# State transfers issued by SyncE, and part of VectorE's work in the mLSTM state loop given to GpSimd

## The reference

```python
# per sample and head: state C is 512 x 512
C_new = decay * C + einsum('k,v->kv', wg * k, v)          # the samples' states, written out
h     = einsum('k,kv->v', q, C_new) / max(|den|, exp(-m))  # the samples' output
C_p   = einsum('sk,sv->kv', wg * k, v)                     # the prompt's state, written out
hc    = num / max(|den|, exp(-m))                          # the prompt's output, per head
mu, var = hc.mean(-1), mean((hc - mu)**2)
hn  = (hc - mu) * rsqrt(var + EPS) * ln_g
out = ((hn + skip * xc) * silu(z)) @ w_out
```

## Time and profile before

| | us |
|---|---|
| median of 3 runs | 2687.95 (2685.96 to 2688.54) |
| profiled execution | 2686.03 |
| its span, first to last instruction | 2683.9 |
| TensorE busy | 2429.1 |
| VectorE busy | 1805.6 |
| ScalarE busy | 1563.1 |
| GpSimd busy | 411.5 |

### The profile page before, as it was taken

One profiled execution on the slowest core, in us unless ns is written; L12 is line 12 of the kernel. 1 busy time (PEld: TensorE's weight loads), 2 busy tenths in 40 slices (PEclk: granted clock), 3 DMA queues, 4 the chain that ended last, 5 costly groups with the idle time before them and its releaser, 6 DMA issues. The chain is left out here.

```text
span 2683.9 us, 50227 instructions
## 1 busy us (share of the span) xinstructions
PE 2429.1 (91%) x17500; PEld 2195.1 (82%) x17500; DVE 1805.6 (67%) x3814; ACT 1563.1 (58%) x3012; POOL 411.5 (15%) x436
## 2 busy tenths in 40 slices
PE   6978999899977999998989978899999987999997
PEld 3658989888966999997766535898899976999997
DVE  6855698866698555557447784459885479655555
ACT  5644555577688555555526762355556569555554
POOL 0000344300043000000002331024440025000000
PEclk8989999999999999999998998999999999999999
DMA  6743444477601545453326995344444520445452
GB/s 231 259 134 141 157 157 157 173 258 259 234 16 33 187 174 185 178 182 133 98 80 265 417 324 185 129 156 157 157 170 172 186 80 0 151 178 184 176 186 96
DMA packets 74318, 455.79 MB, mean 170 GB/s; under 512 B 9680, under 2 KB 9888, under 8 KB 27632
## 3 DMA queue, kind: packets, MB, share of 16 engines
q1 hardware_dynamic: 52128, 379.61, 39.3%
q0 software_dynamic: 20336, 73.30, 7.3%
q10 hardware_dynamic: 1760, 1.68, 0.2%
HBM read 415.28 MB, written 39.27 MB: 169 GB/s over the span
## 5 line engine op out<-in xcount | busy, mean ns | idle before, releaser
L861 ACT ACTIVATE w_parts<-ring 128x512 fp32r<-128x512 f32 x1376 | 853.1, 632 | 804.2 <-PE ps L446 769.9
L1294 DVE TENSOR_TENSOR w_parts<-ring,w_parts 128x512 fp32r<-128x512 f32 x1232 | 853.9, 704 | 613.0 <-ACT w_parts L861 603.7
L446 PE MATMUL ps<-h_hi,w_parts 128*128 128x264 f32 x5376 | 1024.9, 289 | 84.9 <-DVE w_parts L1294 59.4
L446 PEld LDWEIGHTS ps<-h_hi,w_parts 128*128 128x128 f32 x5376 | 857.5, 192 | 114.7 <-issue 60.7
L446 PE MATMUL ps<-h_lo,w_parts 128*128 128x264 f32 x2688 | 771.9, 287 | 0.0
L446 PE MATMUL ps<-g_parts,w_parts 128*128 128x264 f32 x6144 | 748.5, 284 | 6.7 <-DVE g_parts L1594 6.7
L446 PEld LDWEIGHTS ps<-g_parts,w_parts 128*128 128x128 f32 x6144 | 748.2, 189 | 7.1 <-issue 7.1
L446 PEld LDWEIGHTS ps<-h_lo,w_parts 128*128 128x128 f32 x2688 | 516.6, 192 | 2.0
L1197 POOL TENSOR_TENSOR w_parts<-ring,w_parts 128x512 fp32r<-128x512 f32 x144 | 211.7, 1471 | 479.0 <-ACT w_parts L861 478.7
L861 ACT ACTIVATE SCR<-SCR 128x128 f32<-128x128 f32 (+3 forms) x540 | 212.5, 484 | 13.2 <-POOL SCR L1212 8.9
L446 PE MATMUL ps<-SCR 128*128 128x128 f32 x1056 | 155.8, 293 | 63.0 <-DVE SCR L1565 44.8
(11 more groups left out here) (188 smaller groups left out, 1569.4 us busy)
## 6 DMA issues: line engine op xcount, KB each, us to landing
ring<-in_stream SPq DMA_DIRECT2D x362, 1024.0 KB, 4.8
BIG<-in_C POOLq DMA_DIRECT2D x64, 512.0 KB, 8.6
out_C_s<-BIG POOLq DMA_DIRECT2D x64, 512.0 KB, 8.1
out_C_p<-SCR POOLq DMA_DIRECT2D x16, 256.0 KB, 7.5
x<-in_x ACTq DMA_DIRECT2D x1, 1056.0 KB, 15.3
out_y<-BIG POOLq DMA_DIRECT2D x1, 1056.0 KB, 4.2
consts<-in_consts ACTq DMA_DIRECT2D x1, 256.0 KB, 10.8
BIG<-in_gates POOLq DMA_DIRECT2D x1, 192.0 KB, 2.6
```

The lines of the kernel that those rows point to most:

```text
L446: return nc.tensor.matmul(out, lhsT, rhs, start=start, stop=stop, skip_group_check=shared)
L861: return nc.scalar.activation(to, of, f, **kw_)
L1294: tt(w_lo[:, j % HALVES, :], half_of(n, half), w_hi[:, j % HALVES, :].bitcast(F32), ALU.subtract).then_inc(lo_ready[half], 1)
```

## The change

The reciprocal of the denominators is taken head by head, each before its head's product. In the state loop:

- Loads and stores of the states and the store of `Cst` are issued by SyncE, in the same order with the same waits; the weight stream's SyncE program is cut up so that eight of its pairs are issued inside that sequence, one behind each store of `Cst`. `Cst` has one buffer instead of two.
- VectorE still adds the second terms of q C, into three buffers (`rd` with two, `rd_more`); GpSimd adds the two units' sums, and TensorE multiplies once for each iteration.
- The second half of each gate tile's low part is subtracted by GpSimd (`low_z`).
- VectorE joins the gain with the scaling at m = 24 and 25 (one instruction for each chunk); adding the skip part and multiplying with the gate is done by GpSimd, two chunks at a time (`finish_h`), from m = 25 on. ScalarE scales xc by `skip` at m = 16 to 23, two chunks at a time.

```diff
@@ sync @@
+            def rounds_of_pairs(first, end):
+                with sp.Fori(first, end) as r:
+                    for s in range(PAIRS):
+                        sp.wait_ge(pairs_used, r * PAIRS + (s - PAIRS + 1))
+                        pair(r * PAIRS + s, s)
+            def pairs(first, end):
+                for n in range(first, end):
+                    sp.wait_ge(pairs_used, n - PAIRS + 1)
+                    pair(n, n % PAIRS)
+            def load_C(u):
+                sp.dma_start(flat(Cbuf[u % CBUFS]), half_C(C_d, u)).then_inc(C_in[u % CBUFS], 16)
+            z0 = FIRST["ml_z"] // 2
+            ahead = z0 + PAIRS - 1
+            rounds_of_pairs(1, ahead // PAIRS)
+            pairs(ahead // PAIRS * PAIRS, ahead)
+            sp.wait_ge(qs_ready, 2)
+            sp.wait_ge(st_done, 1)
+            for u in range(CBUFS):
+                load_C(u)
+            LAG = 3
+            for u in range(UNITS):
+                sp.wait_ge(C_new, u + 1)
+                sp.dma_start(half_C(C_s_o, u), flat(Cbuf[u % CBUFS])).then_inc(C_out[u % CBUFS], 16)
+                if u % 4 == 3:
+                    n = u // 4
+                    sp.wait_ge(cp_copied, n + 1)
+                    sp.dma_start(C_p_o[n], Cst).then_inc(cp_stored, 16)
+                    if n < KM // 2:
+                        pairs(ahead + n, ahead + n + 1)
+                old = u - LAG
+                if old >= 0 and old + CBUFS < UNITS:
+                    sp.wait_ge(rd_ready, old + 1)
+                    sp.wait_ge(C_out[old % CBUFS], 16 * (old // CBUFS + 1))
+                    load_C(old + CBUFS)
+            ahead += KM // 2
+            again = -(-ahead // PAIRS)
+            pairs(ahead, again * PAIRS)
+            rounds_of_pairs(again, rounds)
+            pairs(rounds * PAIRS, NTILES // 2)
...
@@ tensor, read_C @@
-                for q in range(2):
-                    pe.wait_ge(rd_ready, 2 * m + q + 1)
-                    last = mm(ps[0:HEADS * NSMP, 4, :], one_col[:, at:at + HEADS * NSMP], rd[:, q, :],
-                              m == 0 and q == 0, m == NSMP * HEADS - 1 and q == 1)
-                    last.then_inc(C_read, 1)
+                pe.wait_ge(rd_summed, m + 1)
+                mm(ps[0:HEADS * NSMP, 4, :], one_col[:, at:at + HEADS * NSMP], rd[m % 2],
+                   m == 0, m == NSMP * HEADS - 1).then_inc(C_read, 1)
...
             pe.wait_ge(mly_ready, 1)
+            pe.wait_ge(hn_gated, KM // 2)
             residual_out("ml_out", hT, KM)
...
@@ scalar, scale_rd and the loop @@
+                act.wait_ge(C_new, 2 * m + 1)
+                if m >= 2:
+                    act.wait_ge(C_read, m - 1)
+                func(rd[m % 2], Cbuf[2 * m % CBUFS][:, 0, :], ACT.Copy, scale=qs[:, hd * HC, b:b + 1])\
+                    .then_inc(rd_scaled, 1)
+                act.wait_ge(C_new, 2 * m + 2)
+                if m >= 1:
+                    act.wait_ge(rd_summed, m)
+                func(rd_more, Cbuf[(2 * m + 1) % CBUFS][:, 0, :], ACT.Copy, scale=qs[:, hd * HC + 2, b:b + 1])\
+                    .then_inc(rd_scaled, 1)
...
-                    if n >= 2:
-                        act.wait_ge(cp_stored[n % 2], 16 * (n // 2))
-                    func(Cst[:, n % 2, :], ps[:, 5 + n % 2, :], ACT.Copy).then_inc(cp_copied, 1)
-                if m < KM:
-                    func(xc[:, m, :], xc[:, m, :], ACT.Copy, scale=col("ml_skip", m)).then_inc(skip_ready, 1)
+                    if n >= 1:
+                        act.wait_ge(cp_stored, 16 * n)
+                    func(Cst, ps[:, 5 + n % 2, :], ACT.Copy).then_inc(cp_copied, 1)
+                if KM <= m < KM + KM // 2:
+                    for c in (2 * (m - KM), 2 * (m - KM) + 1):
+                        func(xc[:, c, :], xc[:, c, :], ACT.Copy, scale=col("ml_skip", c)).then_inc(skip_ready, 1)
...
@@ gpsimd @@
+            def low_z(k):
+                j = HALF["ml_z"] + 2 * k + 1
+                pool.wait_ge(hi_ready, j + 1)
+                nc.gpsimd.tensor_tensor(w_lo[:, j % HALVES, :], half_of(FIRST["ml_z"] + k, 1),
+                                        w_hi[:, j % HALVES, :].bitcast(F32), ALU.subtract).then_inc(lo_ready[1], 1)
+            def sum_rd(m):
+                pool.wait_ge(rd_ready, 2 * m + 2)
+                nc.gpsimd.tensor_tensor(rd[m % 2], rd[m % 2], rd_more, ALU.add).then_inc(rd_summed, 1)
+            def finish_h(k):
+                pool.wait_ge(hn_ready, 2 * k + 2)
+                pool.wait_ge(skip_ready, KM)
+                of = (slice(None), slice(2 * k, 2 * k + 2), slice(0, NPR))
+                nc.gpsimd.tensor_tensor(hT[of], hT[of], xc[of], ALU.add).then_inc(hn_skipped, 1)
+                pool.wait_ge(hn_skipped, k + 1)
+                nc.gpsimd.tensor_tensor(hT[of], hT[of], z[of], ALU.mult).then_inc(hn_gated, 1)
+            pool.wait_ge(lo_ready[1], HALF["ml_z"] // 2)
+            for k in range(2):
+                low_z(k)
+            for m in range(NSMP * HEADS):
+                if m >= 1:
+                    sum_rd(m - 1)
+                if 1 <= m < KM - 1:
+                    low_z(m + 1)
+                if m > AT_SCALE:
+                    finish_h(m - AT_SCALE - 1)
+            sum_rd(NSMP * HEADS - 1)
+            for k in range(NSMP * HEADS - AT_SCALE - 1, KM // 2):
+                finish_h(k)
...
@@ vector @@
-            link(vec.reciprocal(flat(em), flat(em)))
             for hd in range(HEADS):
+                link(vec.reciprocal(em[:, hd, :], em[:, hd, :]))
                 dve.wait_ge(num_done, hd + 1)
...
-                low(FIRST["ml_z"] + k, HALF["ml_z"] + 2 * k)
+                low(FIRST["ml_z"] + k, HALF["ml_z"] + 2 * k, halves=1)
...
-                    low(FIRST["ml_z"] + m + 1, HALF["ml_z"] + 2 * m + 2)
+                    low(FIRST["ml_z"] + m + 1, HALF["ml_z"] + 2 * m + 2, halves=1)
...
-                        ph = part.rearrange("p (a c) t -> p a c t", a=2)
-                        link(tt(ph, ph, hs_.unsqueeze(2).to_broadcast([P, 2, HC, NPR]), ALU.mult))
-                    if m == AT_SKIP + i:
-                        dve.wait_ge(skip_ready, KM)
                         for c in range(8 * i, 8 * i + 8):
-                            last = stt(hT[:, c, 0:NPR], hT[:, c, 0:NPR], col("ml_ln_g", c), xc[:, c, 0:NPR],
-                                       ALU.mult, ALU.add)
-                        link(last)
-                    if m == AT_Z + i:
-                        dve.wait_ge(z_ready, KM)
-                        tt(part, part, z[:, 8 * i:8 * i + 8, 0:NPR], ALU.mult)
+                            stt(hT[:, c, 0:NPR], hT[:, c, 0:NPR], col("ml_ln_g", c), hstd[:, c // HC, :],
+                                ALU.mult, ALU.mult).then_inc(hn_ready, 1)
```

More of the change, by code:

```diff
@@ L228, in decoder_step @@
         xm_twice = scr(4096, KM, 2 * NSMP)
-        rd = scr(0, 2, MHD)
-        Cst = scr(1024, 2, MHD)
+        rd = [scr(0, MHD), scr(MHD, MHD)]
+        rd_more = scr(2 * MHD, MHD)
+        Cst = scr(3 * MHD, MHD)
         hsq = scr(2048, KM, NPR)
@@ L323, in decoder_step @@
         cp_copied = sem("cp_copied")
-        cp_stored = [sem(f"cp_stored{i}") for i in range(2)]
+        cp_stored = sem("cp_stored")
         sbc_done = sem("sbc_done")
@@ L340, in decoder_step @@
         rd_ready = sem("rd_ready")
+        rd_summed = sem("rd_summed")
+        hn_ready = sem("hn_ready")
+        hn_skipped = sem("hn_skipped")
+        hn_gated = sem("hn_gated")
         C_read = sem("C_read")
@@ L418, in _ @@
                 pair(n, n)
-            rounds = NTILES // 2 // PAIRS
[L420 to L427, removed]
+            def rounds_of_pairs(first, end):
[3 more added lines that the diff above has]
+                        pair(r * PAIRS + s, s)
@@ new lines, in pairs, with half_C, flat @@
+            def pairs(first, end):
+                for n in range(first, end):
+                    sp.wait_ge(pairs_used, n - PAIRS + 1)
+                    pair(n, n % PAIRS)
+            def half_C(C, u):
+                return C[u // 2][:, u % 2 * 2 * MHD:(u % 2 + 1) * 2 * MHD]
+            def flat(v):
+                return v.rearrange("p a b -> p (a b)")
+            def load_C(u):
+                sp.dma_start(flat(Cbuf[u % CBUFS]), half_C(C_d, u)).then_inc(C_in[u % CBUFS], 16)
+            rounds = NTILES // 2 // PAIRS
@@ L952, in peer @@
                     act.wait_ge(stores, 16 * 6)
-                    for i in range(2):
-                        act.wait_ge(cp_stored[i], 16 * KM // 2)
+                    act.wait_ge(cp_stored, 16 * KM)
                     for i in range(CBUFS):
@@ L1238, in _ @@
             pool.dma_start(m_o, mrow[0:HEADS, NPR - 1:TOK]).then_inc(stores, 16)
[L1239 to L1242, removed]
             pool.wait_ge(sqn_ready, 1)
             pool.dma_start(n_s_o, nst).then_inc(stores, 16)
[L1245 to L1248, removed]
-                if u % 4 == 3:
-                    n = u // 4
-                    pool.wait_ge(cp_copied, n + 1)
```

(17 more changed lines are left out.)

11 lines of the change are left out of this document (4 added, 7 removed).

## The result

The changed kernel takes 2697.53 us (median of 6 runs, 2692.3 to 2698.02) against 2687.95: a ratio of 1.0035, 95% interval 1.0025 to 1.0044. It is slower by some 9.6 us where 3.6 less were forecast.

A forecast was written before the change was run, and what follows sets the result against it. Transfers and TensorE were taken to bound the first half, a chain through the prompt product the second. Terms -8.0 - 1.0 + 5.4 = -3.6 took 2687.95 to 2684.4 us, own range 2679 to 2689.

The forecast's parts named there:

- Reciprocal by heads: Ahead of the state loop: four short reciprocals replace one of 6.55 us, so the first update comes earlier, -8.0 us.
- Transfers on SyncE: State loop: loads and stores moved from GpSimd to SyncE, past the weight stream, make no engine wait longer, 0 us.
- The rival of one queue: All transfers on SyncE's queue move less, 360 GB/s, making first-half pairs 15.2 us: +17, 2701 us; chance 0.15.
- First half: Iterations below 16: TensorE's work shrinks but transfers keep a pair at 13.06 us; only the ramp gains, -1.0 us.
- Second half: Iterations 16 to 31: longer chain and skip scalings outweigh VectorE's relief, +5.4 us, between 0 and +10.
- The hop: Second half, even iterations: with GpSimd's addition ahead, TensorE's read ends at +6.45 instead of +5.33, +1.1 us.
- the last term: Iteration 26 to the copy of the sums: 40.2 us with a low-clock start against 40.45, -0.2, between -5.3 and +4.4.
- Finishing on GpSimd: Last iterations: GpSimd's finishing of the prompt's output lies beside them, 0 us; 1.3 for each add pushed back.
- VectorE's relief: Rival: some 18 us of work off VectorE in the loop pays in full, 2673 us; chance 0.2.
- GpSimd and VectorE stretching each other: Rival: first-half add and low half slow each other, +0.5 a pair, +4, time stays at 2688 us; chance 0.2.
- The signs named ahead: If right: update near 1419, first-half pairs near 13 us, DMA 1.0, TensorE not full, later waits for ScalarE and GpSimd.
- the 400 named as a mark: First half: a transfer rate under 400 GB/s (or over 425) would show the forecast wrong.

The follow-up runs named there:

- six matmuls: The changed kernel with six more unread matmuls on TensorE in every even iteration from the 18th on, ahead of its wait for GpSimd's sum: 2690.5 us.
- the finishing held: The changed kernel with both sums read by TensorE, no addition on GpSimd, and GpSimd's finishing made to wait for the previous iteration's sums: 2672.4 us.
- the sum read twice: The changed kernel with the addition kept and TensorE reading its result a second time against columns of zeros, result unchanged: 2704.95 us.

## Why the prediction was wrong, point by point

*Reciprocal by heads, -8.0.* Right: 8.2 in the timeline, 7.9 alone.

*Transfers on SyncE, 0.* Right: 2685.9 with nothing else changed. The rival of one queue is out; SyncE's queue carried 420 GB/s in the pair that begins at 1492.27. ScalarE's waits in the loop name no prompt store, so the single staging buffer cost nothing either.

*First half, -1.0.* The size held (-0.2 in the profiled execution), the working only in part. The prediction took 13.06 us a pair as what transfers need. Pairs 4 to 10 of after took 12.34, with a DMA share of 1.00 to 1.03 at 370 to 405 GB/s: TensorE's work did get shorter, and the pairs moved 4.6 to 5.0 MB each instead of the 5.47 counted. But that is no proof that transfers set nothing. With the product ahead of the read, where the chain is shorter still, pairs came back to 13.2 and 13.3 us with TensorE not full, and ScalarE waited 7.4 us for state loads from 1492.02 to 1518.49:

```profile
1492.02:1505.27 13.25, 10.77 (x62) 7.31 (x60) 9.48 (x14) 10.05 (x15) 5.77 (x4) 1.00 1.02 418
```

In after the gain of 0.7 a pair was lost in the first pair and in two of 14 to 15 us at a clock of 0.88.

*Second half, +5.4.* This is the step that failed, in its size: +18.5. The hop was right: with the clock at 1.00 pairs 22 and 28 took 12.97 and 10.63 to 10.64 with the addition and 11.80 and 9.48 without it, 1.2 each against the 1.1 predicted. What failed is the clock under which iterations 16 to 25 were priced. The prediction took its terms there at full clock, from rows of before at 1.00, and a low start from 26 on. Each addition came between VectorE's sums and TensorE's read, the clock was low in seven of eight prompt products, and read, column sums and product took 6.43 us (pair 28) instead of 3.45 (the same pair with six matmuls) or the 3.35 of the prediction. Measured against the terms: iterations 16 to 19 +3.4 (+1.1 predicted), 20 and 21 +5.0 (+2.0), 22 and 23 +3.9 (+1.1), 24 and 25 +1.7 (+1.4), 26 to the copy +4.6 (-0.2). Of these, 24 and 25 are VectorE's (busy 21.38 of 21.45 us) and not the clock's. For the last term the prediction had worked out +4.4 with all at the low clock, and kept it only as a bound. It knew the mechanism for the end of the loop and didn't ask whether its own edit would bring it to the rest. A second thing is hidden behind the low clock: its 13.9 us for the last two iterations at full clock was too short, since they took 16.93 at 0.93 with six matmuls.

*Finishing on GpSimd, 0.* Right as a term in after: the two additions that it pushed back, by 1.1 us each (they began at 1610.94 and 1638.11), lay beside slow products of TensorE, which ended at 1613.6 and 1640.9. Once the clock was back it did cost, at the end of the loop (the 16.93 us above). Its scheduling was luck: the addition itself kept it away from the gains.

*The rivals.* VectorE's relief didn't pay in full, since the chain decided. *GpSimd and VectorE stretching each other* is not what made after long (addition 1.27 us in the median, 1.66 at most; gains 504 ns against 478). It is real all the same: gains of 1106 ns where the finishing ran beside them, and in after itself two sums of 2.41 us instead of 1.41 at iteration 29. *One hardware queue* named the time that came nearest, 2701, but by a mechanism that didn't occur.

*The signs named ahead.* First update near 1419, TensorE no longer full in the first half, VectorE waiting longer for ScalarE (5.55 us ahead of iteration 28, 4.59 ahead of 30) and TensorE's reads waiting for GpSimd: right. The view of waits of TensorE in the loop of after (us in total, times, longest):

```profile
PE ps L493 <- POOL SCR L1295: 54.1, 17, 8.3
```

Before had waited 28.2 us, in 10 waits, for VectorE there. The first half moved 379 GB/s, under the 400 named as a mark against the forecast; but before itself had moved 390 there, with its state transfers in GpSimd's queue, so the mark could tell nothing. The copy of the sums came 230.0 us after the first update, beyond the 215 named as the mark of a wrong forecast.

## What to carry to other kernels

When an edit puts a wait ahead of TensorE in a loop where its matmuls lie on the critical chain, price the chain at both levels of the clock, and don't take the level from a trace whose waits the edit will lengthen; here 1.2 us of hop became 3 to 5 us a pair. Taking half of its reads off TensorE gained nothing behind such a wait, and unused work in the wait gained 12 us; better still was to order its queue so that the product that others wait for doesn't stand behind the one that has to wait. Before two edits are kept together, ask which of them holds the other in place: without the addition, the finishing fell upon VectorE.

## What the runs showed of the hardware

- The prompt product (four matmuls, 128x512) took 1.96 us at a granted clock of 1.00 and 3.37 to 3.76 at 0.50 to 0.58 (2.4 and 1.2 GHz). Ahead of the seven slow ones in the second half of after TensorE had waited 3.5 to 8.3 us. The length of the wait alone doesn't tell: behind waits of 5.97 us in before, 6.56 in the kernel with the finishing held and 7.09 with the sum read twice, the read of four matmuls took 3.4 to 3.6 us and the product behind it 1.96; behind one of 4.92 in before both were slow (3.62 and 3.76).
- GpSimd's additions and products of two SBUF tensors and VectorE's instructions on SBUF tensors slow each other. Without the addition VectorE's gains took 1106 ns instead of 480, beside GpSimd's 1.44 and 1.33 us instead of 1.27; in after single products of GpSimd took up to 2.43 us.
- A DMA share of 1.00 to 1.03 stood beside 370 as well as 420 GB/s: the share alone doesn't tell the rate.
